# Differential-attention scores as three rounded products, and the attention loop reordered

## The reference

```
def _sdpa(q, k, v, scale):
    s = jnp.einsum('bqhd,bkhd->bhqk', q, k).astype(F32) * scale
    p = jax.nn.softmax(s, axis=-1).astype(v.dtype)
    return jnp.einsum('bhqk,bkhd->bqhd', p, v)

def _diff_sdpa(q1, q2, k1, k2, v, scale, lam):
    p1 = jax.nn.softmax(jnp.einsum('bqhd,bkhd->bhqk', q1, k1).astype(F32) * scale, axis=-1)
    p2 = jax.nn.softmax(jnp.einsum('bqhd,bkhd->bhqk', q2, k2).astype(F32) * scale, axis=-1)
    return jnp.einsum('bhqk,bkhd->bqhd', (p1 - lam * p2).astype(v.dtype), v)
```

## Time and profile before

| | |
|---|---|
| median of 3 runs | 2948.03 us (2946.21 to 2948.14) |
| time of the profiled execution | 2947.06 us |
| its span | 2945.3 us |
| TensorE (PE) busy | 2846.3 us, 97% |
| VectorE (DVE) busy | 1678.3 us, 57% |
| ScalarE (ACT) busy | 881.7 us, 30% |
| PE in the chain that ended last | 93% |

### The profile page before, as it was taken

How to read it: one execution, slowest core, us unless ns; L and a number is a source line. 1 busy time by engine, 2 the same in 40 slices (tenths; PEclk the granted TensorE clock), 3 DMA queues, 4 the chain that set the end, 5 groups by cost and what they waited for, 6 DMA issues and landing times.

```text
span 2945.3 us, 43839 instructions
## 1 busy us (share of the span) xinstructions
PE 2846.3 (97%) x16950; PEld 2433.6 (83%) x16950; DVE 1678.3 (57%) x3117; ACT 881.7 (30%) x1370; POOL 106.6 (4%) x82
## 2 busy tenths in 40 slices
PE   6999999999988999999999999999999988999998
PEld 4888888888756788888888888888888756898996
DVE  5876677733467578767776335443434476543443
ACT  4221122233256442211222321122233355422222
POOL 0000000043000000000000000000024000000000
PEclk8999999999999999999999999999999999999999
DMA  6444344322300134433442213221222200233232
GB/s 224 126 126 126 100 124 131 109 63 58 81 1 1 29 93 136 129 118 106 127 123 89 64 58 116 70 64 57 69 72 71 76 1 1 83 89 100 87 102 68
DMA packets 422759, 255.39 MB, mean 87 GB/s; under 512 B 26017, under 2 KB 418057, under 8 KB 422666
## 3 DMA queue, kind: packets, MB, share of 16 engines
q1 hardware_dynamic: 422160, 254.00, 28.9%
q10 hardware_dynamic: 506, 0.13, 0.0%
HBM read 252.01 MB, written 2.10 MB: 86 GB/s over the span
## 4 chain that ended last, share of the span: by engine, by line
PE 93%; DVE 3%; ACT 3%; issue 1%; DMA 0%; SPq 0%; DVEq 0%; ACTq 0%
PE pair L685 56%; PE pair L679 26%; PE pair L902 2%; PE pair L948 2%; ACT buf L1229 1%; PE pair L651 1%; PE pair L916 1%; PE pair L880 1%; PE pair L933 1%; DVE neg_max L1672 1%; PE pair L925 1%; PE pair L862 1%; DVE lo_w L1362 0%; PE pair L868 0%; PE pair L873 0%
## 5 line engine op out<-in xcount | busy, mean ns | idle before, releaser
L685 PE MATMUL pair<-n_hi,hi_w 128*128 128x260 f32 (+2 forms) x3456 | 846.8, 325 | 19.6 <-DVE n_lo L1401 13.5
L685 PE MATMUL pair<-n_lo,hi_w 128*128 128x256 f32 (+1 forms) x3456 | 844.2, 324 | 0.0
L685 PE MATMUL pair<-n_hi,lo_w 128*128 128x258 f32 (+2 forms) x3456 | 844.1, 325 | 0.0
L685 PEld LDWEIGHTS pair<-n_hi,hi_w 128*128 128x128 f32 x3456 | 531.6, 189 | 83.0 <-issue 11.0
L685 PEld LDWEIGHTS pair<-n_hi,lo_w 128*128 128x128 f32 x3456 | 536.1, 190 | 58.4
L685 PEld LDWEIGHTS pair<-n_lo,hi_w 128*128 128x128 f32 x3456 | 534.0, 189 | 54.9
L1362 DVE TENSOR_TENSOR lo_w<-raw_w,hi_w 128x1024 fp32r<-128x1024 f32 (+1 forms) x296 | 394.3, 1332 | 302.3 <-ACT hi_w L1028 301.5
L1028 ACT CAST hi_w<-raw_w 128x1024 fp32r<-128x1024 f32 (+1 forms) x296 | 328.8, 1111 | 653.2 <-PE pair L685 365.1
L1534 DVE SCALAR_TENSOR_TENSOR mod_acc<-mod_w,silu_c,mod_acc 128x256 f32<-128x256 f32 x896 | 364.6, 478 | 0.0
L1457 DVE TENSOR_TENSOR buf<-pair,rstd 128x512 f32<-128x512 f32 (+1 forms) x308 | 164.7, 570 | 309.1 <-PE pair L685 309.1
L679 PE MATMUL pair<-h_hi,hi_w 128*128 128x512 f32 x1232 | 338.8, 345 | 0.0
(11 more groups left out here) (186 smaller groups left out, 1981.4 us busy)
## 6 DMA issues: line engine op xcount, KB each, us to landing
raw_w<-in_ffn_w SPq DMA_DIRECT2D x176, 512.0 KB, 3.8
mod_w<-in_w_mod SPq DMA_DIRECT2D x64, 1024.0 KB, 5.1
raw_w<-in_ffn_w SPq DMA_DIRECT2D x64, 704.0 KB, 4.7
raw_w<-in_w_in SPq DMA_DIRECT2D x38, 512.0 KB, 3.9
raw_w<-in_w_out SPq DMA_DIRECT2D x16, 512.0 KB, 4.0
pro_scale<-in_w_mod SPq DMA_DIRECT2D x2, 2048.0 KB, 16.3
pro_shift<-in_w_mod SPq DMA_DIRECT2D x2, 2048.0 KB, 13.0
x_tok<-in_x SPq DMA_DIRECT2D x4, 512.0 KB, 5.6
```

Source lines behind the costliest of these rows:

```text
L685: mm = pe.matmul(pair[s][:, a:a + m], wt[:, k * P:(k + 1) * P], src[:, of(k):of(k) + m], start=opens, stop=closes)
```

## The change

- **Scores.** Queries and keys of the differential heads are split in a high and a low part. high_dqk (ScalarE) copies a tile into an F32R tile that is free at the time (dqk_hi_tile), low_dqk (VectorE) writes tile minus high part over the tile itself (proj_r is proj seen as F32R). scores_diff does three rounded products for each half row and head, in the order (hi, hi), (hi, lo), (lo, hi), with the heads' halves s in the inner loop; before, it did one plain f32 product.
- **Where the splits stand.** There are eight tiles j: even j is the query tile of head j // 2, odd j its key tile. j = 0 to 3 are split in the task stage, the high parts behind the tasks in DQK_AFTER, the low parts behind the next rotations. j = 4 to 7 (heads 2 and 3) are split at the end of the steps 1, 3, 5 and 7 of the loop. Query tiles have 512 columns in layer 1, all others 768.
- **Banks.** The sums of values_diff move from pair[1] to pair[0], those of values_mla from pair[0] to pair[1]; with them the exponential that each waits for changes.
- **Order on TensorE.** values_mla comes last in an odd iteration, behind values_diff and transposes_mla. **On VectorE** the pt_d copy comes between the first two maxima, and low_mla behind the second and inverse_mla. **On ScalarE** in even iterations the pt_m copy stays ahead of the third exponential; in odd ones turn_inverse and the pt_m copy come behind it.
- **Inverse sums.** inverse_mla makes one column (inv_sum) in place of 64 equal ones; values_mla turns it in two products of 64 columns that read it broadcast.

The new semaphores dqk_hi and dqk_lo are left out below.

```
@@ -156,6 +156,7 @@
+DQK_AFTER = [("v", 3), ("vm", 0), ("vm", 1), ("vm", 2)]
@@ -226,6 +227,7 @@
+        rstd_r, = overlay(("rstd_r", TOK, F32R))
         rstd = sb("rstd", TOK)
@@ -253,6 +255,7 @@
+        proj_r, = overlay(("proj_r", T_IN * TOK, F32R))
         proj, v_mla = overlay(("proj", T_IN * TOK, F32), ("v_mla", (TOK // P) * 256, F32))
@@ -262,7 +265,6 @@
-        inv_wide = [wk_n[:, i * 2 * MV:(i + 1) * 2 * MV] for i in range(2)]
@@ -434,13 +438,29 @@
             i = 2 * (c % N_SLOT) + s if s < 2 else 2 * N_SLOT + c % N_SLOT
             return slice(i, i + 1)
+        def dqk_tile(j, tensor=proj):
+
+            return tile(tensor, (T_DQ, T_DK)[j % 2] + j // 2)
+
+        def dqk_hi_tile(j):
+
+            if j < 4:
+                return n_lo[:, (KD // 2 + j) * TOK:(KD // 2 + j + 1) * TOK]
+            if j == 7:
+                return n_hi[:, 6 * TOK + 6 * MV:7 * TOK + 6 * MV]
+            return rstd_r[:, :] if j == 6 else tile(proj_r, T_POOL + j - 4)
+
+        def dqk_rope(j):
+
+            return TASKS.index(("rope", (T_DQ, T_DK)[j % 2] + j // 2, "d"))
+
         def acc_mla(L, c):
-            return pair[0][:, TOK:1024] if c < N_STEPS[L] - 1 else pair[2][:, P:3 * P]
+            return pair[1][:, TOK:1024] if c < N_STEPS[L] - 1 else pair[2][:, P:3 * P]
         def acc_diff(L, c):
-            return pair[1][:, TOK:TOK + P] if c < N_STEPS[L] - 1 else pair[2][:, 0:P]
+            return pair[0][:, TOK:TOK + P] if c < N_STEPS[L] - 1 else pair[2][:, 0:P]
         def task_pair(a):
@@ -644,15 +664,17 @@
                 else:
                     if st0 + c > 1:
                         pe.wait_ge(o_mla, (st0 + c) // 2)
-                    pe.wait_ge(exp_done[0], st0 + c + 3)
+                    pe.wait_ge(exp_done[1], st0 + c + 3)
                 for a in range(nk // P):
                     kt = k0 // P + a
                     for e in range(2):
                         pe.matmul(acc[MV * e:MV * (e + 1), 0:P],
                                   v_mla[:, kt * 256 + (h - 1 + e) * MV:kt * 256 + (h + e) * MV],
                                   pt_m[e][:, a * P:(a + 1) * P], start=(a == 0), stop=(a == nk // P - 1))
-                pe.matmul(acc[:, P:2 * P], inv_wide[(st0 + c) // 2 % 2], ident[:, :], start=True, stop=True)\
-                  .then_inc(pv_mla, 1)
+                for e in range(2):
+                    mm = pe.matmul(acc[MV * e:MV * (e + 1), P:2 * P],
+                                   inv_sum[:, slot(c - 1 + e, 2)].broadcast_to([P, MV]), ident[:, :], start=True, stop=True)
+                mm.then_inc(pv_mla, 1)
             def turn_diff(L, h, n):
@@ -889,6 +911,7 @@
                 def scores_diff(c):
                     h, at, k0, nk = steps[c]
+                    pe.wait_ge(dqk_lo, 2 * (L * HEADS + h + 1))
                     for s in range(2):
                         if st0 + c:
                             pe.wait_ge(exp_done[s], st0 + c)
@@ -897,12 +920,14 @@
                             pe.wait_ge(o_mla, st0 // 2 + c // 2 - 1)
                         if a and c >= 2:
                             pe.wait_ge(o_diff, st0 + c - 1)
-                        for s in range(2):
-                            rows_s = slice(DDIM * s, DDIM * (s + 1))
-                            mm = pe.matmul(pair[s][:, a:a + m], tile(proj, T_DQ + h, P, at)[rows_s, :],
-                                           tile(proj, T_DK + h, m, k0 + a)[rows_s, :], start=True, stop=True)
-                            if a + m == nk:
-                                mm.then_inc(s_ready[s], 1)
+                        q, k = ([dqk_hi_tile(j), dqk_tile(j, proj_r)] for j in (2 * h, 2 * h + 1))
+                        for n, (i, j) in enumerate(((0, 0), (0, 1), (1, 0))):
+                            for s in range(2):
+                                rows_s = slice(DDIM * s, DDIM * (s + 1))
+                                mm = pe.matmul(pair[s][:, a:a + m], q[i][rows_s, at:at + P],
+                                               k[j][rows_s, k0 + a:k0 + a + m], start=(n == 0), stop=(n == 2))
+                                if a + m == nk and n == 2:
+                                    mm.then_inc(s_ready[s], 1)
                 def scores_mla(c):
@@ -942,7 +967,7 @@
                     else:
                         if st0 + c:
                             pe.wait_ge(o_diff, st0 + c)
-                        pe.wait_ge(exp_done[1], st0 + c + 2)
+                        pe.wait_ge(exp_done[0], st0 + c + 2)
                     for a in range(nk // P):
                         kt = k0 // P + a
                         mm = pe.matmul(acc_diff(L, c), pt_d[:, a * P:(a + 1) * P],
@@ -957,11 +982,11 @@
                         transposes_diff(c - 1)
                     if c < n_steps:
                         scores_mla(c)
-                    if c % 2 and c >= 3:
-                        values_mla(L, c - 2)
                     if c:
                         values_diff(c - 1)
                         transposes_mla(c - 1)
+                    if c % 2 and c >= 3:
+                        values_mla(L, c - 2)
             for q, w in enumerate(SWEEPS):
                 if starts_norm(w):
@@ -1181,6 +1206,12 @@
                 if w["what"].endswith("_up"):
                     cnt["h"] += FG
+            def high_dqk(L, j):
+
+                n = TOK if j % 2 or L < DEPTH - 1 else SEQ
+                act.wait_ge(out_dve, L * N_DVE + read_out("d", dqk_rope(j) + 1))
+                act.copy(dqk_hi_tile(j)[:, 0:n], dqk_tile(j)[:, 0:n]).then_inc(dqk_hi, 1)
+
             def mixer(L):
                 w_last = [w for w in SWEEPS if w["layer"] == L and w["what"] == "in"][-1]
                 more = L < DEPTH - 1
@@ -1213,6 +1244,8 @@
                             ins = act.activation(of(2 * arg + e, m)[0:NOPE, :], src[NOPE * e:NOPE * (e + 1), 0:m],
                                                  ACT.Identity, scale=SC_MLA if what == "uq" else 1.0)
                     ins.then_inc(out_act, 1)
+                    if (what, arg) in DQK_AFTER:
+                        high_dqk(L, DQK_AFTER.index((what, arg)))
                     if what == "uq" and arg == 2:
                         act.wait_ge(out_dve, L * N_DVE + read_out("d", TASKS.index(("rope", T_KR, "d")) + 1))
@@ -1237,6 +1270,14 @@
                     act.activation(o_diff_at(h, at), acc, ACT.Identity, scale=inv_sum[:, slot(c, 0)])
                     act.activation(squares[:, c % 6 * P:(c % 6 + 1) * P], acc, ACT.Square,
                                    scale=inv_sum[:, slot(c, 0)], accum_out=sub_sum[:, c:c + 1]).then_inc(o_diff, 1)
+
+                def probabilities_mla(c):
+
+                    nk = steps[c][3]
+                    act.wait_ge(t_mla, st0 + c + 1)
+                    if st0 + c > 1:
+                        act.wait_ge(pv_mla, (st0 + c) // 2)
+                    act.copy(pt_m[c % 2][:, 0:nk], pair[3][:, 0:nk]).then_inc(pt_mla, 1)
                 def turn_inverse(c):
@@ -1260,18 +1301,20 @@
                         high_mla(c - 3)
                     if c < n_steps:
                         exponential(c, 1)
-                    if c % 2 and c >= 3:
-                        turn_inverse(c - 2)
                     if c:
                         out_diff(c - 1)
-                        act.wait_ge(t_mla, st0 + c)
-                        if st0 + c > 2:
-                            act.wait_ge(pv_mla, (st0 + c - 1) // 2)
-                        act.copy(pt_m[(c - 1) % 2][:, 0:steps[c - 1][3]], pair[3][:, 0:steps[c - 1][3]]).then_inc(pt_mla, 1)
+                    if c and c % 2 == 0:
+                        probabilities_mla(c - 1)
                     if c < n_steps:
                         if c:
                             act.wait_ge(t_mla, st0 + c)
                         exponential(c, 2)
+                    if c % 2:
+                        if c >= 3:
+                            turn_inverse(c - 2)
+                        probabilities_mla(c - 1)
+                    if c in (1, 3, 5, 7):
+                        high_dqk(L, 4 + c // 2)
                 act.wait_ge(o_diff, st0 + n_steps)
                 act.activation(sub_sum[:, 0:n_steps], sub_sum[:, 0:n_steps], ACT.Ln, bias=eps_col[:, 0:1],
                                scale=1.0 / DIFF_V).then_inc(sub_ready, 1)
@@ -1635,6 +1678,13 @@
                         ins = dve.tensor_copy(mla_q(h, nq_all)[NOPE:, :], q_rot[h * ROPE:(h + 1) * ROPE, 0:nq_all])
                 ins.then_inc(out_dve, 1)
+            def low_dqk(L, j):
+
+                n = TOK if j % 2 or L < DEPTH - 1 else SEQ
+                dve.wait_ge(dqk_hi, 2 * HEADS * L + j + 1)
+                dve.tensor_tensor(dqk_tile(j, proj_r)[:, 0:n], dqk_tile(j)[:, 0:n],
+                                  dqk_hi_tile(j)[:, 0:n].bitcast(F32), ALU.subtract).then_inc(dqk_lo, 1)
+
             def mixer(L):
                 w_last = [w for w in SWEEPS if w["layer"] == L and w["what"] == "in"][-1]
```

(21 more changed lines are left out.)

## The result

The changed kernel takes 2930.43 us (median of 5 runs, 2928.43 to 2933.27) against 2946.21 us for the kernel before in the same runs: a ratio of 0.9946, with a 95% interval of 0.9931 to 0.9960. That is 15.8 us less; forecast were 13.8 less. The profiled execution has a span of 2928.3 us, 17.0 less than before.

What follows compares the result with a forecast made beforehand. TensorE, busy for 97% of the span, was taken to bound the kernel. Steps at -24.1 us and loop splits at +10.3 made -13.8 us, so 2934.5 us, range 2927 to 2949.

Steps and rivals of the forecast that it cites:

- Three rounded products: scores_diff: two heads' products run side by side, 1.06 us of work in place of about 1.28, 0.22 us less.
- Rival (a): scores_diff: rounded products of the two halves don't run side by side, scores cost 2.12 us, total 2958 us; chance 0.12.
- Twelve loads in file: scores_diff: if its weight loads don't overlap, an estimate of 1.28 us, no gain, and a whole sum of about -10 us.
- The even step: Plain even loop step over 768 keys: 6.77 us falls to 5.86; with low_mla, 7.44 falls to the same 5.86.
- The stall for o_mla: Each even step: second half of scores_diff waits for the o_mla only just made, a stall of 0.2 us.
- The bank swap: Even steps: values_diff waits for the first exponential instead, so the chain loses one exponential, 0.89 us.
- The odd step: Odd loop step, TensorE-bound: 7.59 us less 0.22 for scores and 0.07 for the inverse, 7.30 us.
- Splits in the task stage: Task stage of each layer: four copies and four subtractions fit into idle time, TensorE waits for none, cost nothing.
- Splits in the loop: Steps 1, 3, 5, 7: low_dqk delays the next step's first maximum by 1.37 us; +10.3 us over both layers.
- Rival (c): Loop: idle time at the splits halves TensorE's clock, about 12 us in all, result 2946; chance 0.13 with other small mishaps.
- The sum: Whole kernel: -24.1 us from the steps, +10.3 us for the splits in the loop, together -13.8 us.
- the first pairs: First steps of the loops: 0.2 us of scores in each, 0.9 of the exponential after the very first; 2.4 us.

Runs made afterwards that it cites:

- e1: Changed kernel with the plain f32 scores of before and no splits, so only order, banks and inverse: 2923.73 us, ratio to before 0.9928.
- e3: Changed kernel with all eight splits in the task stage, none in the loop: 2919.33 us, ratio to before 0.9914.
- e4: Changed kernel with the two loops of scores_diff exchanged, three products of half 0, then three of half 1: 2934.18 us, single run.
- e9: Changed kernel with the old banks and the pt_d copy behind the second maximum on VectorE, as before: 2969.12 us, single run.
- e5: Changed kernel with the old banks, values_diff again behind the second exponential, in the new order: 3021.79 us, ratio to before 1.0259.
- e2: Kernel before plus rounded products and splits where the change has them, with old order, banks and inverse: 2968.33 us, ratio to before 1.0074.
- e7: Kernel before plus rounded products, with all eight splits in the task stage and old order, banks and inverse: 2943.35 us, ratio 0.9985.

## Why the prediction was right, step by step

- **Three rounded products, -0.22 us.** Right. scores_diff went from 1.49 to 1.25 us, 1.27 forecast. e1 against e3, which differ in the products and early splits alone, has it at 0.17 us in an even and 0.24 in an odd step and 4.4 us in all. Rival (a), no sharing and 2.12 us, falls; e4 shows sharing even with the halves apart. The twelve loads don't limit either. Timeline after, weight loads of the first six:

```profile
928.20 0.53 PEld L927 LDWEIGHTS pair<-proj_r 64*128 64x128 f32 x6 [0.17 <-issue]
```

  They take 0.53 us, and four of them 0.30, as before.

  Twelve loads in file, by the Trainium skill, TensorE: Matmul & The Clock Gate, section "LDWEIGHTS (loading the stationary operand)", would be an estimate of 1.28 us, and six of them 0.64. The trace sides with its "Part 3: Packing small matmuls": the six take 0.53 us, and all of scores_diff 1.25 with its changeover.
- **The even step, 5.86.** It is 5.70. The stall for o_mla was over-sized: 0.06 us (1.31 against 1.25), not 0.2. Without it the chain is shorter than TensorE's work, which is then the bound. With this the late even steps brought 1.07 us for the plain and 1.7 for those with low_mla, where I had 0.91 and 1.58.
- **The bank swap as the loss of one exponential, 0.89 us.** Right from the order of before, and e9 has 0.95 us of waiting with it undone. But swap and copy order hang together: with the copy ahead of the second maximum and the old banks it is 1.79 us (e5). The prediction didn't see that the new VectorE order would be a loss without the swap.
- **The odd step, 7.30.** 7.32. The inverse was put at -0.07 us; e1 leaves 0.03 for it and the order together.
- **Splits in the task stage at nothing.** Right, to within 1 us. From the last product of the projection to the first scores_diff, layer 0 took 48.3 us before, 48.0 after and 48.4 in e3, which puts four more there. Layer 1 took 42.8, 43.9 and 43.5, and 44.5 in e1, which has no splits at all. The extra four of e3 cost about 1 us in the first steps of the loops, not here.
- **Splits in the loop, +10.3 us.** Right in place, mechanism and size: 1.30 us where I had 1.37, and 10.0 to 11.1 us by e3. Step by step against e3 they are 4.7 us in layer 1, as forecast, and 6.8 in layer 0 where I had 5.6. The excess is mostly at the first context step, where the clock fell: of the 2.5 us over the same step of e3 (5.32), 1.35 are values_diff at the lower clock.
- **Rival (c), the clock.** It happened once in the loops after the first steps (at 888 us), not eight times; e4 has the same fall at the same step. e2 and e5 show what their expectations had left out: with gaps of 2.5 to 3.7 us in the steps behind a split (e2) or of 1.79 us and more in nearly every step over 768 keys (e5), the granted clock of the loop is 0.89 and 0.85, and lost time is lost twice. The Trainium skill, TensorE: Matmul & The Clock Gate, section "Part 1: The HAM clock gate", lets an idle TensorE fall to half its clock. The traces agree on the level (0.50), but here TensorE had been idle only for 1.55 us, after a wait of 0.61 us, with work between and behind.
- **The sum.** Without the splits I had -24.1 us, and e3 has -25.8. By the steps of e3's trace the plain even ones brought 6.8 us (6.4 forecast), those with low_mla 10.3 (9.5), the odd ones 3.3 (3.8), the first pairs 2.6 (2.4) and the context steps 2.5 (2.0). So the terms were each within 1 us, and their errors partly cancel. The first pairs are the least sure: step 1 of layer 0 took 6.25 us after and 8.06 in e3, where two subtractions stand ahead of the first maximum and the clock was at 1.2 GHz until about 841 us. Two side sums of the prediction don't come out: the first steps as itemised make 2.1 us, or 3.0 if each loop has a very first step, not 2.4; and a scores term of nothing would leave about -8 us (26 steps at 0.22 us), not -10.

The parts don't quite add up. Against before, order, banks and inverse alone give -21.4 us, the products alone with early splits -2.3, all together -25.8 (e3). On top of the new order the products bring 4.4 us. In the old order they shorten the steps just as much (6.77 to 6.53, 7.44 to 7.20, 7.59 to 7.36), but the waits before values_diff stay at 0.95 and 1.59 us and the clock falls in three long steps. That the clock took the difference is read from one trace of e7; how much it took in the timed runs isn't shown.

## What to carry to other kernels

A part whose work fits into idle time can still cost more than its work: ask what stands behind its wait in the same queue. Here 0.95 us of subtraction, queued ahead of a maximum, held TensorE for 1.3 us, and most of the same work in the stage before cost nothing (e3). When a rearrangement and an arithmetic saving come together, time each alone: here the rearrangement gave more than the whole, and the arithmetic alone, with its splits in place, made the kernel slower. Take the waits out before shortening the work between them: with the waits left in place, the clock took back a good part of the saving in the trace of e7.

## What the runs showed of the hardware

- Rounded products over partitions 0 to 63 and 64 to 127, accumulated in different banks, run side by side also when they are issued as two separate groups (e4: 1.32 us; after: 1.31).
- The length of a gap alone didn't decide whether the clock fell. The kernel before waits 1.59 us before values_diff in six steps and the product took 1.60 us each time; e7 has the same six waits with less work between them, and the clock fell at three (2.42 to 2.76 us for the product). After the change, gaps of 0.9 to 1.5 us in the even steps 2 to 8 left it at 2.4 GHz, and it fell once, at the gap of 1.55 us.
- The loss from waits on a busy TensorE rose faster than the waits. From the first scores_diff to the last of each loop, TensorE is idle for 73 us in e5 and 46 in e9, at a mean granted clock of 0.86 to 0.87 against 0.92 to 0.94. So e5 has 27 us more of idle time there, and its loops are 48 us longer (one trace each).
